# Expert gate and up weights in eight places of 1 MB instead of four of 2 MB, in a one-core diffusion layer

## The reference, cut to what matters

```python
def expert_block(args):
    tok, e = args
    xb = t_pad[tok]                                   # rows of the tokens of this block
    hdn = jax.nn.silu(xb @ w_gate[e]) * (xb @ w_up[e])  # w_gate[e], w_up[e]: 2048 x 512
    return hdn @ w_down[e]                            # w_down[e]: 512 x 2048
```

## Time and profile before

| | |
|---|---|
| median of 3 runs | 2075.7 us (2072.02, 2077.52, 2075.7) |
| profiled execution, its own time | 2074.03 us |
| its span in the trace | 2072.5 us |
| TensorE busy | 1980.5 us, 96% of the span |
| VectorE, ScalarE busy | 1218.4 us (59%), 525.4 us (25%) |
| moved by DMA | 654.10 MB, mean 316 GB/s over the span |
| granted TensorE clock, mean | 0.996 |

### The profile page before, as it was taken

How to read it: one execution, slowest core, us unless ns; L and a number is a source line. 1 busy time by engine, 2 the same in 40 slices (tenths; PEclk the granted TensorE clock), 3 DMA queues, 4 the chain that set the end, 5 groups by cost and what they waited for, 6 DMA issues and landing times.

```text
span 2072.5 us, 28682 instructions
## 1 busy us (share of the span) xinstructions
PE 1980.5 (96%) x10495; PEld 1210.9 (58%) x10496; DVE 1218.4 (59%) x2017; ACT 525.4 (25%) x620; POOL 60.8 (3%) x119
## 2 busy tenths in 40 slices
PE   5789999999999999999999999999999999999998
PEld 2468888888888888877887433333333333333332
DVE  2459989998989898988975233332233333333223
ACT  4242434243434434344555100000000000000000
POOL 0000000000000000001000000000000000000000
PEclk9999999999999999999999999999999999999999
DMA  9985585868685858697854999999999799999997
GB/s 356 348 274 166 176 254 183 259 186 240 192 250 175 273 165 265 183 336 253 301 207 203 367 425 426 428 426 426 425 428 426 302 420 426 425 427 427 425 425 323
DMA packets 293261, 654.10 MB, mean 316 GB/s; under 512 B 13580, under 2 KB 188080, under 8 KB 260576
## 3 DMA queue, kind: packets, MB, share of 16 engines
q1 hardware_dynamic: 284240, 626.87, 80.8%
q0 software_dynamic: 8016, 26.40, 3.9%
q10 hardware_dynamic: 960, 0.23, 0.1%
HBM read 642.81 MB, written 10.65 MB: 315 GB/s over the span
## 4 chain that ended last, share of the span: by engine, by line
PE 28%; DMA 24%; DVE 1%; issue 0%; ACT 0%; SPq 0%; DVEq 0%; ACTq 0%
DMA wt<-in_moe_w_down 24%; PE bank L2127 9%; PE bank L2101 7%; PE bank L1919 7%; PE bank L2074 2%; PE bank L2081 1%; PE bank L2044 1%; PE bank L1978 0%; DVE x L1659 0%; DVE x1l L1507 0%; PE bank L2111 0%; PE bank L1859 0%; ACT xgT L948 0%; DVE onehot L1578 0%; DVE x L1431 0%
## 5 line engine op out<-in xcount | busy, mean ns | idle before, releaser
L2101 PE MATMUL bank<-wt,xe 128*64 128x512 f32 x1984 | 448.7, 597 | 34.2 <-DMA wt<-in_moe_w_up 26.2
L1799 PE MATMUL bank<-hTh,whi 128*128 128x256 f32 (+1 forms) x1232 | 394.0, 340 | 0.0
L1800 PE MATMUL bank<-hTl,whi 128*128 128x256 f32 (+1 forms) x1232 | 388.0, 335 | 0.0
L2101 PEld LDWEIGHTS bank<-wt,xe 128*64 128x64 f32 x1984 | 133.1, 136 | 320.7 <-issue 246.2
L1667 DVE SCALAR_TENSOR_TENSOR gsil<-gtanh,bank 128x256 f32<-128x256 f32 x32 | 13.5, 421 | 424.9 <-ACT gtanh L959 424.9
L1799 PEld LDWEIGHTS bank<-hTh,whi 128*128 128x128 f32 x1232 | 233.5, 189 | 26.3 <-issue 2.7
L1800 PEld LDWEIGHTS bank<-hTl,whi 128*128 128x128 f32 x1232 | 233.6, 190 | 23.5
L2127 PE MATMUL bank<-wt,hdn 128*64 128x512 f32 x1024 | 231.8, 598 | 2.1 <-DVE hdn L1672 0.6
L1806 PE MATMUL bank<-hTh,wlo 128*128 128x256 f32 (+1 forms) x1232 | 225.3, 335 | 0.0
L1659 DVE TENSOR_TENSOR x<-x,bank 128x512 f32<-128x512 f32 x256 | 161.5, 684 | 87.5 <-PE bank L2074 87.5
L1806 PEld LDWEIGHTS bank<-hTh,wlo 128*128 128x128 f32 x1232 | 191.8, 190 | 23.7
(11 more groups left out here) (321 smaller groups left out, 2003.6 us busy)
## 6 DMA issues: line engine op xcount, KB each, us to landing
wt<-in_moe_w_gate SPq DMA_DIRECT2D x62, 2048.0 KB, 23.3
wt<-in_moe_w_up SPq DMA_DIRECT2D x62, 2048.0 KB, 24.6
wt<-in_moe_w_down SPq DMA_DIRECT2D x62, 2048.0 KB, 20.7
raw<-in_ssm_w_in SPq DMA_DIRECT2D x77, 1024.0 KB, 5.8
raw<-in_ada_w SPq DMA_DIRECT2D x70, 1024.0 KB, 6.4
raw<-in_ssm_w_out SPq DMA_DIRECT2D x32, 1024.0 KB, 5.8
fr<-in_ada_w SPq DMA_DIRECT2D x18, 1024.0 KB, 12.7
bc<-cum_d POOLq DMA_DIRECT2D x32, 512.0 KB, 5.2
```

What stands on the lines that cost most here:

```text
L1799: pe.matmul(bank[:, 0:width], wh[:, k, :], hTh[:, k, 0:width], start=(k == 0), stop=False)
L1800: last = pe.matmul(bank[:, 0:width], wh[:, k, :], hTl[:, k, 0:width], start=False, stop=False)
L2101: last = pe.matmul(GATE_UP[h][SLOTS * c:SLOTS * c + SLOTS, :], rows[:, k, :], wt[j][:, FF * i:FF * i + FF], start=(k < 2), stop=(k >= KC - 2))
```

## The change

Gate and up get eight places of 1 MB, with four chunks each: `QW` is 4, `NQ` is 4. Place 2q holds chunks 4q to 4q+3 of gate, place 2q+1 the same of up. A partition's part of such a load is 8 KB in one piece. The eight places lie in the same 64 KB per partition as the four before. Down keeps its two places and its loads. The waits ahead of the loads of expert 0 move with the memory that they guard. Since `s_wt` now needs ten semaphores, others are saved: three of the side tiles use semaphores of front tiles that are done by then (with counts that go on from theirs), and the pair `s_dh` becomes one semaphore that counts to two per block. `turned(b, 0)` stands in the middle of the last place as before, which is now after two of its four chunks.

```diff
-    QW = KC // 2
-    NQ = 2
+    QW = KC // 4
+    NQ = 4
...
-        wt = [at(f"wt{j}", kb, [P, 2 * D]) for j, kb in enumerate((88, 104, 152, 168, 120, 0))]
+        wt = [at(f"wt{j}", kb, [P, D]) for j, kb in enumerate((88, 96, 104, 112, 152, 160, 168, 176))]
+        wt += [at(f"wt{2 * NQ + w}", kb, [P, 2 * D]) for w, kb in enumerate((120, 0))]
...
-        s_side136 = sem("s_side136")
-        s_side128 = sem("s_side128")
         s_side160 = sem("s_side160")
-        s_side144 = sem("s_side144")
...
-        s_dh = [sem(f"s_dh{h}") for h in range(2)]
+        s_dh = sem("s_dh")
...
+        s_side136, s_side144, s_side128 = s_fr[4], s_fr[5], s_fr[7]
+        LAND136, LAND144, LAND128 = (FCOUNT[FLAST[slot]] for slot in (7, 8, 10))
...
             for j in range(2 * NQ):
-                if j == 2:
+                if j == 4:
                     sp.wait_ge(s_ssq, 8)
                     sp.wait_ge(s_x1a, 4 * TT)
                     sp.wait_ge(s_rprep, 3)
-                if j == 3:
+                if j == 6:
                     sp.wait_ge(s_logit, TT)
                 up_gate(slice(0, 1), j)
...
-                for h in range(2):
-                    dve.wait_ge(s_dh[h], b + 1)
+                dve.wait_ge(s_dh, 2 * b + 2)
...
-                                last.then_inc(s_dh[h], 1)
+                                last.then_inc(s_dh, 1)
```

More of the change, by code:

```diff
@@ L445, in build @@
         SPLIT160 = [side160[:, 0, :], side160[:, 1, :], side172[:, 0, :], side172[:, 1, :]]
-        SIDE = {0: (WHOLE136, s_side136, 16), 1: (WHOLE128, s_side128, 16), 2: (SPLIT160, s_side160, 32), 3: (WHOLE128, s_side128, 32),
-                4: (WHOLE136, s_side136, 32), 5: (WHOLE144, s_side144, 16), 6: (WHOLE136, s_side136, 48), 7: (WHOLE144, s_side144, 32)}
+        s_side136, s_side144, s_side128 = s_fr[4], s_fr[5], s_fr[7]
+        LAND136, LAND144, LAND128 = (FCOUNT[FLAST[slot]] for slot in (7, 8, 10))
+        SIDE = {0: (WHOLE136, s_side136, LAND136 + 16), 1: (WHOLE128, s_side128, LAND128 + 16), 2: (SPLIT160, s_side160, 32),
+                3: (WHOLE128, s_side128, LAND128 + 32), 4: (WHOLE136, s_side136, LAND136 + 32), 5: (WHOLE144, s_side144, LAND144 + 16),
+                6: (WHOLE136, s_side136, LAND136 + 48), 7: (WHOLE144, s_side144, LAND144 + 32)}
         def ring(g, kind, n):
```

## The result

| | before | changed kernel |
|---|---|---|
| median of 14 runs each | 2073.61 us | 2079.88 us |
| lowest and highest | 2071.94, 2077.52 | 2078.24, 2085.03 |
| profiled execution, own time | 2074.03 us | 2078.24 us |
| span in the trace | 2072.5 us | 2076.7 us |

The ratio is 1.0031, with a 95% interval of 1.0024 to 1.0038: 6.3 us more, where 11.8 were forecast. The direction was right, the size was not. The forecast of 2087.5 us also stood on a median of three runs (2075.7); fourteen runs have 2073.61, so 2.1 us of the 7.6 between forecast and measurement are that. 2079.88 lies inside the range (2079.2 to 2092.0), 0.7 us from its low end, and only by the 2.5 us that the range adds for the spread of a median, since the low sum was 2075.7 + 6.0 = 2081.7.

A forecast was written before the change was run, and what follows sets the result against it. The rate of the loads was taken to bound the expert part. Pieces +11.6, restart 0, start 0 and transpose +0.2 made +11.8 us on a 2075.7 median, so 2087.5 us, range 2079.2 to 2092.0.

The forecast's parts named there:

- What bounds the kernel: Expert part: runs at the rate of the loads, in two continuous stretches; longer loads are paid in each cycle.
- the price of a cycle: Gate and up loads: 8 KB pieces instead of 16 KB cost 0.40 us per expert, +11.6 us over 29 cycles.
- the one by TensorE's waits: Estimate of the 8 KB pieces' cost from landings that TensorE sees: 0.31 us per expert, lower end 0.2.
- The reading by durations: Estimate of the 8 KB pieces' cost from packets' own durations, 616 and 315 ns: 0.47 us per expert.
- The small addition for the completions of more loads: Gate and up, eight loads for four: completion packets lift the price from 0.38 to 0.40 us per expert.
- The restart: After the two-block expert: first load up to 1.74 us sooner, but down's issue holds the stream; 0 us.
- The start: First stretch: expert 1's gate load released up to 1.74 us sooner, but queued behind other loads; 0 us.
- The transpose: Gate's transpose in the two-block expert's second block: TensorE waits for ScalarE's copy, delaying down's issue; +0.2 us, once.
- the item on what costs nothing: Whole expert part: added waits, SP issues and shared semaphores cost nothing; the tail behind the last down load is unchanged.
- A: Gate and up loads: down's lower rate comes from its distant rows, not packet size; no change, 2075.9 us; chance 0.13.
- B: Behind the two-block expert: earlier release carries through, second stretch begins 1.7 us sooner; 2085.3 us; chance 0.05.
- C: All added loads: each costs a fixed time of its own, 13.2 us per expert; 2459 us; chance 0.02.

The follow-up runs named there:

- e3_two_loads: Kernel before, each of its four 2 MB places filled by two loads of 1 MB, old release kept: 2081.7 us against 2072.29, ratio 1.0038.
- e4_down16: Kernel before with down in 16 KB pieces per partition and strided weight loads in the transposes: 2084.89 us against 2072.31, ratio 1.0061.
- e9_down16_copy: Kernel before with down in 16 KB pieces, the stride in ScalarE's copy, transposes unchanged: 2068.12 us against 2072.84, ratio 0.9977.
- e1_pieces8: Kernel before, old places and loads, each gate and up load fetching two 8 KB pieces per partition: 2080.99 us against 2072.29, ratio 1.0043.

## Why the prediction was half right, point by point

**What bounds the kernel** held: two continuous stretches of loads, 16 and 13 cycles. The count fits: 16 x 0.29 us is the +4.6 of the first.

**The step that failed is the price of a cycle**, in the item on the pieces of 8 KB. It took 0.40 us, and 0.29 was measured, so 29 cycles cost 8.4 and not 11.6: 3.2 of the 5.5 us by which the forecast change was too large. The mechanism was right and the term was mis-sized. Of its three readings the one by TensorE's waits (0.31) was nearly exact, and the two that I weighed more were too high. They could have been tested against rows that were there. 19.50 us for gate and up at 430.2 GB/s and 4.194 MB / 422.0 = 9.94 us for down make 29.44, and the period is 29.53. Since down's 422 proved right (the changed kernel moves everything at 422), gate and up must have taken 29.53 - 9.94 = 19.59, and 19.88 - 19.59 is 0.29. The windows inside gate and up read too high, because the count in 14 us hangs on where the edges fall. Moved by 0.4 us, one of them reads 427 in place of 430 (kernel before):

```profile
1452.00:1466.00 14.00, 13.63 (x64) 4.30 (x62) 4.17 (x7) 0.00 (x0) 0.00 (x0) 1.00 1.01 430
1452.40:1466.40 14.00, 13.63 (x64) 4.27 (x62) 3.86 (x6) 0.00 (x0) 0.00 (x0) 1.00 1.00 427
```

Nine such windows 0.2 us apart in each of three cycles read 427 to 431, 428.9 in the mean, which is 19.56 us for gate and up and a price of 0.32. The reading by durations (0.47) adds up what the profile gives as a packet's time. Those times overlap (shares of 101.0 and 101.1%, more than there is), but taking that off leaves 0.44; what else makes it too high stays open. The small addition for the completions of more loads (0.38 to 0.40) had nothing behind it either: those packets cost nothing that can be seen. A fixed price of 9.4 ns for 32 more packets is 0.30.

The Trainium skill, DMA: Bandwidth & Descriptors, section Why small descriptors are slow, names a fixed overhead per packet of about three cycles and 32 bytes of metadata per operation, and holds joining descriptors into packets to be worth it up to 256 bytes only. No run here joins any, and none shows that the measured price is that overhead. Here some 9 ns for each piece are worth 7 us even between 8 and 16 KB, since some 900 us of the kernel run at the rate of the engines.

**The restart** was right (0 us): issue of gate 2.12 us after the block's start, down unmoved, and e3_two_loads with the old release as long as the changed kernel. **The start** gave nothing, as forecast: the first stretch is longer by its 16 cycles and nothing else.

**The transpose** was forecast at +0.2 us and cost none. The step counted its chunks wrongly: with places of four chunks gate's last chunk is the 28th and not the 24th, and the transpose stands behind the 30th and not the 26th. Both shift by the same 1.74 us, so the 0.2 us of the forecast was, by luck, not touched by it. The 0.34 us from the end of ScalarE's copy to the next transpose, taken from the other copy, is no lower limit: TensorE follows the gate copy, which ends at 1650.02, at 1650.16, in 0.14 us:

```profile
1649.42 0.60 ACT L958 ACTIVATE gsb<-bank 128x512 f32<-128x512 f32 x1 [25.65 <-PE bank L2101]
```

**The rest.** 0.6 us at the end of the second stretch and 0.6 at the stores came back that no step had (the item on what costs nothing left the tail unchanged): 8.4 less these is the +7.3 of the profile. The medians have about 1 us less than that, inside their interval. With the 3.2 of the price and the 0.2 of the transpose this is the whole distance from 11.8 to 6.3, to the rounding. **The rivals:** A is refuted by the changed kernel's own 422 GB/s, B by the unmoved down issue, C by the period.

## What to carry to other kernels

When the loads bound a kernel, a split load costs what its added packets cost: here about 9 ns per packet and engine. Look first at how long the contiguous piece per partition is, since a new layout of one operand (down's 8 KB to 16 KB) may give more than finer places do. Where two rates are read from windows, let their times add up to a period that is known exactly before the difference is used. A finer release pays only where that release ends the wait, so follow the stream to the next issue that holds it; and a cost that each block pays must be summed over all blocks, even if each block still hides it.

## What the runs showed of the hardware that was not expected

- A fixed price per packet, 9.1 to 9.4 ns, that 4, 8 and 16 KB packets share, in a stream without gaps.
- Weight loads whose columns lie 16 bytes apart (e4_down16) take 327 ns, not 191, in the mean (groups of lines, 1200 to 1600 us, before and then e4_down16):

```profile
L2081 PEld LDWEIGHTS bank<-tri_lo,gsb 128*128 128x128 f32 x224 | 27.1, 191 | 22.0 <-issue 11.4 <-ACT gsb L962 10.6
```

```profile
L2081 PEld LDWEIGHTS bank<-tri_lo,gsb 128*128 128x128 f32 x222 | 53.9, 327 | 22.0 <-issue 11.4 <-ACT gsb L962 10.6
```

  The same stride costs ScalarE nothing when it reads the bank (0.60 us in e9_down16_copy and before).
- SP's issue of a load, 0.33 us elsewhere, takes up to some microseconds behind others in the queue. In the changed kernel at 1411 us, and with pieces of 4 KB:

```profile
1411.13 3.53 SPq L601 DMA_DIRECT2D wt<-in_moe_w_gate  x1
```

```profile
1478.89 8.06 SPq L600 DMA_DIRECT2D wt<-in_moe_w_gate  x1
```

  The cause is not shown: e1_pieces8 has the changed kernel's pieces in half as many loads, and none of its gate and up issues takes over 0.7 us. It cost nothing here, since the engines stayed occupied (shares of 101.3 and 102.1% over 1200 to 1600 us). A kernel in which SP has other work behind such an issue may pay for it; no run tests that.
